# Six accumulator banks in the feed-forward loop, and the sample states' products placed in the output projection

## The chip, the cores and the metric

The kernel is written in Bass and runs on one core of one Trainium2 chip. A time is the device time of one execution in microseconds (us). The core has five instruction streams that run beside each other and wait for each other through semaphores: TensorE (PE, with its weight loads shown as PEld), VectorE (DVE), ScalarE (ACT), GpSimd (POOL) and SyncE (SP, which here only issues transfers). TensorE's granted clock has two levels, 2.4 GHz (shown as 1.00) and 1.2 GHz (shown as 0.50).

## The reference

One inference step of a decoder trunk with two layers, 1024 prompt tokens and 8 samples of 4 new tokens (1056 columns in all), model width 1024, feed-forward width 2816, all in fp32. Each layer computes

```
h = rmsnorm(x);  z = h @ w_in
o_gla = gated linear attention of 4 heads (key 64, value 128), with a recurrent state
o_swa = sliding-window attention of 8 query heads over 2 key/value heads
x = x + [o_gla ; o_swa] @ w_o
h = rmsnorm(x);  x = x + (silu(h @ w_gate) * (h @ w_up)) @ w_down
```

and a last rmsnorm gives the outputs. The gated linear attention also returns its recurrent states. For the prompt that is one state per layer. For the samples the new state of each sample is `exp(b_last) * S + k_dec^T v`, 8 samples by 4 heads of a 64 x 128 matrix. The sum `k_dec^T v` of these 32 small matrices is what the steps `sample_states` (the products) and `sample_sum` (scaling the old state and adding the products) compute. Nothing later in the layer reads these states: they are only stored.

## The kernel before, in words

All activations lie transposed, 128 channels by 1056 tokens, in eight channel tiles k = 0..7. The tokens are cut into three column tiles tt of 384, 384 and 288. A weight unit is 1024 x 128 weights (512 KB). SP loads it into `w_raw` (a ring of two), POOL splits it into a high part `w_hi` and a low part `w_lo` of reduced-precision fp32 (`split`, lines 481 to 506; the low part in pieces of 256 columns), and PE multiplies: for each k three matmuls, high x high, high x low, low x high (`passes`, lines 551 to 557). The activations are split the same way into `h_hi` (ACT) and `h_lo` (DVE, and for k = 1, 4, 7 POOL: `lows`, lines 508 to 515). So a product of one unit with one column tile is a group of 24 matmuls into one PSUM bank.

The order of all work up to the feed-forward part is written out by `schedule()` (lines 73 to 203) as a list of steps, and each engine walks through the same list and does its part of each step. The matmul groups are numbered in this order, group g writes bank `acc[g % 3]`, and `acc_free[b]` counts how often the reader of a bank has released it. `open_group` (line 547) makes PE wait for the release of the group three before.

PSUM has eight banks: `acc0` to `acc2`, `pair_a` (two banks), `pair_b` (two banks) and `single`. The last three serve the attention steps.

The list's end, around which the change lies:

- the output projection: units 19 to 26, three column tiles each. `("z", u, tt)` is PE's group, `("take", u, tt)` is DVE's addition of the bank to x (L1218), then ACT squares it (L858) and DVE adds the square to a running sum (L1158);
- the transition into the feed-forward part (lines 191 to 202): `stat` sums the squares over the channels on PE (L567), `rstd` turns that into 1/rms on ACT (L867, L870), `normed` makes the new h: DVE scales (L1178), ACT writes `h_hi` (L880), DVE or POOL write `h_lo` (L1183, L513). `sample_states` (PE, L793: 32 products with 32 rows, 64 output partitions and 128 columns, each recorded as two matmuls) stands between `stat` of tile 1 and `stat` of tile 2. `sample_sum` (DVE, L1430 and L1434) is the last step. It reads `pair_a` and `pair_b`. SP stores the result (L469) inside the feed-forward loads.

Then the feed-forward loop: 11 rounds (`Fori`, line 799 for PE). A round has 36 groups: four units (gate and up for two feed-forward tiles; 12 groups of 24 matmuls), then two units of w_down (24 groups of 6 matmuls). ACT reads a gate bank (Silu, L1128), DVE an up bank (L1483), DVE adds a w_down bank to x (L1498). Before each group `ff_open` (line 800) waits for the bank's last reader, with the numbering of `acc_free` carried on. In the first unit of the first round PE also waits, k by k, for the h of this column tile (`split_in`, line 812). POOL's order at this place (lines 530 to 538) is: split unit 27, lows of tiles 0 and 1, split unit 28, lows of tile 2, split unit 29.

Of the kernel before, what the change touches and what calls it, by code (L numbers as in the profile page):

```python
# [26 lines left out]
NTT = len(COLS)  # L27
TW = 384
RANK = 16
NCH = SEQ // P  # L30
# [12 lines left out]
POOL_LOWS = (1, 4, 7)  # L43
DVE_LOWS = tuple(k for k in range(KC) if k not in POOL_LOWS)
ACCS = 3
NEG = -1.0e30


# [2 lines left out]
UNITS = U_FF + 6 * FPAIRS  # L51
FF_UNITS = 6
FF_GROUPS = 4 * NTT + KC * NTT


CONSTS = {"ident": 128, "ones": 128, "band": 256, "reset": 32, "bmask": NB,
# [16 lines left out]
def schedule():  # L73
# [3 lines left out]
    steps = []  # L77
# [4 lines left out]
    def normed(n, tt, half=None):  # L82
        return [("normed", n, tt, h) for h in range(2) if half is None or h == half]

    def project(u, tt):
        return [("z", u, tt), ("take", u, tt)]
# [60 lines left out]
    gate = [(u, tt) for u in range(U_GG, U_WO) for tt in range(NTT)]  # L147
# [38 lines left out]
    for k in range(KC - 1):  # L186
        for tt in range(NTT):
            steps += project(U_WO + k, tt)
            if k > 0 or tt > 0:
                squares(1, (tt - 1) % NTT, [k if tt > 0 else k - 1])  # L190
    k, u = KC - 1, U_FF - 1
# [6 lines left out]
    steps += [("z", u, 2)] + normed(1, 0, 0) + [("stat", 1, 1), ("take", u, 2)]  # L198
    squares(1, 2, [k])

    steps += [("sample_states",), ("stat", 1, 2), ("rstd", 1, 1)] + normed(1, 0, 1) + [("rstd", 1, 2)]
    steps += normed(1, 1) + normed(1, 2) + [("sample_sum",)]
    return steps


# [23 lines left out]
def trunk(nc, x_t, units, consts, tables, dec_mask, params, w_gk2, state_in, kcache_t,  # L229
# [100 lines left out]
    pair_b = nc.alloc_psum_tensor("pair_b", [P, 1024], f32)  # L330
    single = nc.alloc_psum_tensor("single", [P, 512], f32)

    def sem(name):
        return nc.alloc_semaphore(name)

# [6 lines left out]

    acc_full = sem("acc_full")
    acc_free = [sem(f"acc_free{b}") for b in range(ACCS)]
    w_loaded = [sem(f"w_loaded{s}") for s in range(RING)]
    w_high = sem("w_high")
    ga_low = sem("ga_low")
# [62 lines left out]
    def bank(g):  # L410
        return acc[g % ACCS]

# [11 lines left out]
    def width(tt):  # L424
        return COLS[tt][1] - COLS[tt][0]
# [20 lines left out]
    with nc.Fori(0, DEPTH) as layer:  # L446
        with nc.Block() as block:
# [98 lines left out]
            def _(pe):  # L546
# [249 lines left out]
                        last.then_inc(ds_full, 1)  # L796


                with pe.Fori(0, FPAIRS) as i:
                    def ff_open(j):  # L800
                        g = G_FF + j
                        pe.wait_ge(acc_free[g % ACCS], i * (FF_GROUPS // ACCS) + g // ACCS)
                        return bank(g)

                    for j in range(4):
                        u = U_FF + j
                        pe.wait_ge(w_ready, i * FF_UNITS + (u + 1))
                        for tt in range(NTT):
                            out = ff_open(NTT * j + tt)[:, 0:width(tt)]
                            for k in range(KC):  # L810
                                if j == 0:
                                    split_in(pe, NTT + tt, k)
                                last = passes(out, u % RING, k, h_hi[:, k, cols(tt)], h_lo[:, k, cols(tt)],
                                              k == 0, k == KC - 1)
                            last.then_inc(acc_full, 1)
                    for j in range(2):
                        u = U_FF + 4 + j
                        pe.wait_ge(w_ready, i * FF_UNITS + (u + 1))
                        for tt in range(NTT):
                            pe.wait_ge(hid_ready, i * (2 * NTT) + (NTT + tt + 1))  # L820
                            for d in range(4):
                                out = ff_open(4 * NTT + 4 * (NTT * j + tt) + d)[:, 0:width(tt)]
                                for f in range(2):
                                    last = passes(out, u % RING, 4 * f + d, hid_hi[:, f, cols(tt)],
                                                  hid_lo[:, f, cols(tt)], f == 0, f == 1)
                                last.then_inc(acc_full, 1)

            @block.scalar
            def _(act):
# [290 lines left out]
                with act.Fori(0, FPAIRS) as i:  # L1120
                    for f in range(2):
                        for tt in range(NTT):
                            w = width(tt)
                            j = 2 * NTT * f + tt
                            g = G_FF + j
                            n_done = NTT * f + tt
                            act.wait_ge(acc_full, i * FF_GROUPS + (g + 1))
                            nc.scalar.activation(silu_g[:, tt, 0:w], bank(g)[:, 0:w], ACT.Silu)\  # L1128
                              .then_inc(acc_free[g % ACCS], 1)
                        for tt in range(NTT):  # L1130
                            w = width(tt)
                            n_done = NTT * f + tt
                            g = G_FF + NTT * (2 * f + 1) + tt
                            act.wait_ge(acc_free[g % ACCS], i * (FF_GROUPS // ACCS) + (g // ACCS + 1))
                            nc.scalar.activation(hid_hi[:, f, cols(tt)], tmp_a[:, n_done % 2, 0:w],  # L1135
                                                 ACT.Copy).then_inc(hid_high, 1)

# [3 lines left out]
            def _(dve):  # L1141
# [324 lines left out]
                with dve.Fori(0, FPAIRS) as i:  # L1466
                    for f in range(2):
                        for tt in range(NTT + 1):
                            if tt < NTT:
                                w = width(tt)  # L1470
                                j = NTT * (2 * f + 1) + tt
                                g = G_FF + j
                                n_done = NTT * f + tt
                                gate = g - NTT
                                dve.wait_ge(acc_free[gate % ACCS], i * (FF_GROUPS // ACCS) + (gate // ACCS + 1))
                                dve.wait_ge(acc_full, i * FF_GROUPS + (g + 1))
                                if n_done >= 2:
                                    dve.wait_ge(hid_ready, i * (2 * NTT) + (n_done - 1))
                                else:

                                    b = G_FF - 1
                                    dve.wait_ge(acc_free[b % ACCS], i * (FF_GROUPS // ACCS) + (b // ACCS + 1))
                                nc.vector.tensor_tensor(tmp_a[:, n_done % 2, 0:w], silu_g[:, tt, 0:w],  # L1483
                                                        bank(g)[:, 0:w], ALU.mult).then_inc(acc_free[g % ACCS], 1)
                            if tt > 0:
                                m = NTT * f + tt - 1
                                w = width(tt - 1)
# [4 lines left out]
                    for j in range(2):  # L1492
                        for tt in range(NTT):
                            for d in range(4):
                                g = G_FF + 4 * NTT + 4 * (NTT * j + tt) + d
                                dve.wait_ge(acc_full, i * FF_GROUPS + (g + 1))
                                xs = x[:, 4 * j + d, cols(tt)]
                                nc.vector.tensor_tensor(xs, xs, bank(g)[:, 0:width(tt)],  # L1498
                                                        ALU.add).then_inc(acc_free[g % ACCS], 1)

        nc.sync.sem_clear(layer_sems)
        nc.all_engine_barrier()
# [163 lines left out]
```

## Time and profile before

| what | value |
|---|---|
| time, median of 3 runs | 2704.58 us (2703.75 to 2707.66) |
| the profiled execution's own time | 2702.21 us |
| its span, first to last instruction | 2700.4 us |
| mean granted TensorE clock | 0.969 |
| PE busy | 2543.7 us, 94% |
| DVE, ACT, POOL busy | 1101.0, 583.3, 870.5 us (41%, 22%, 32%) |
| DMA | 128.66 MB, mean 48 GB/s |

Busy time is that of the records laid over each other, so PE, whose matmuls overlap, is not at its peak where it reads 94%. The span has two equal layers: in the first the output projection runs from about 453 to 551 us, the transition to 583 us, and the feed-forward loop from there to about 1350 us; in the second the transition ends at about 1918 us and the loop at 2674 us. The rest is the final norm and the store.

### The profile page before, as it was taken

The numbers are of one execution on the slowest core, as the hardware profiler recorded it, in microseconds if no ns is written. First come the engines' busy times: TensorE is split into PE (matmuls) and PEld (weight loads), VectorE is DVE, ScalarE is ACT, GpSimd is POOL, SyncE is SP. The second block draws the span as 40 slices with busy tenths as digits, with TensorE's granted clock in tenths as the row PEclk, the third lists the DMA queues.
The fourth block names the chain that finished last, engine by engine and source line by source line (L and its number), as shares of the span: only waits on it lengthen the run. The fifth ranks groups of instructions, "written<-read, shape, count | busy, mean of one in ns | idle before, by whom it ended". The sixth has DMA issues, their size and how long they took to land. (4 is left out here: it accounts for less than half of the span.)

```text
span 2700.4 us, 39407 instructions
## 1 busy us (share of the span) xinstructions
PE 2543.7 (94%) x15202; PEld 2404.5 (89%) x15202; DVE 1101.0 (41%) x2091; ACT 583.3 (22%) x1281; POOL 870.5 (32%) x1344
## 2 busy tenths in 40 slices
PE   3999989989999999999869999999899999999998
PEld 2887778989999999999858867789899999999997
DVE  6635386252222222222366354843522222222224
ACT  3035434130010100101130364441210101010012
POOL 3311112343333333333232211123433333333331
PEclk8999998989999999999969999999899999999999
DMA  4200011111111111111121001011111111111111
GB/s 146 92 24 24 18 38 51 47 47 47 47 39 47 47 47 47 42 43 47 47 97 41 24 24 39 17 64 42 48 47 47 47 47 39 47 47 47 47 39 71
DMA packets 47213, 128.66 MB, mean 48 GB/s; under 512 B 4272, under 2 KB 21872, under 8 KB 46320
## 3 DMA queue, kind: packets, MB, share of 16 engines
q1 hardware_dynamic: 38192, 110.91, 12.5%
q10 hardware_dynamic: 8928, 16.55, 1.7%
q8 instruction: 54, 0.88, 0.1%
q14 instruction: 39, 0.32, 0.0%
HBM read 116.10 MB, written 13.37 MB: 48 GB/s over the span
## 5 line engine op out<-in xcount | busy, mean ns | idle before, releaser
L555 PE MATMUL acc<-h_hi,w_hi 128*128 128x384 f32 (+1 forms) x3360 | 1121.2, 334 | 54.7 <-POOL h_lo L513 29.6
L556 PE MATMUL acc<-h_lo,w_hi 128*128 128x384 f32 (+1 forms) x3360 | 1100.4, 328 | 0.0
L557 PE MATMUL acc<-h_hi,w_lo 128*128 128x384 f32 (+1 forms) x3360 | 1097.9, 327 | 0.0
L555 PEld LDWEIGHTS acc<-h_hi,w_hi 128*128 128x128 f32 x3360 | 643.9, 192 | 95.4 <-issue 39.8
L556 PEld LDWEIGHTS acc<-h_lo,w_hi 128*128 128x128 f32 x3360 | 645.3, 192 | 0.6
L557 PEld LDWEIGHTS acc<-h_hi,w_lo 128*128 128x128 f32 x3360 | 644.1, 192 | 0.0
L487 POOL TENSOR_TENSOR w_hi<-w_raw,const 128x32 fp32r<-128x32 f32 x186 | 50.0, 269 | 1672.9 <-PE acc L557 1600.6
L495 POOL TENSOR_TENSOR w_lo<-w_raw,w_hi 128x256 fp32r<-128x256 f32 x744 | 545.2, 764 | 15.5
L1483 DVE TENSOR_TENSOR tmp_a<-silu_g,acc 128x384 f32<-128x384 f32 x132 | 68.8, 521 | 872.2 <-PE acc L557 872.2
L1498 DVE TENSOR_TENSOR x<-x,acc 128x384 f32<-128x384 f32 (+1 forms) x528 | 272.8, 520 | 203.5 <-PE acc L557 201.4
L555 PE MATMUL acc<-hid_hi,w_hi 128*128 128x384 f32 (+1 forms) x1056 | 342.4, 324 | 0.0
L556 PE MATMUL acc<-hid_lo,w_hi 128*128 128x384 f32 (+1 forms) x1056 | 340.9, 323 | 0.0
L557 PE MATMUL acc<-hid_hi,w_lo 128*128 128x384 f32 (+1 forms) x1056 | 340.4, 322 | 0.0
L1128 ACT ACTIVATE silu_g<-acc 128x384 f32<-128x384 f32 x132 | 61.2, 465 | 848.9 <-PE acc L557 848.8
L557 PEld LDWEIGHTS acc<-hid_hi,w_lo 128*128 128x128 f32 x1056 | 198.3, 188 | 0.0
L556 PEld LDWEIGHTS acc<-hid_lo,w_hi 128*128 128x128 f32 x1056 | 198.3, 188 | 0.0
L555 PEld LDWEIGHTS acc<-hid_hi,w_hi 128*128 128x128 f32 x1056 | 198.2, 188 | 0.0
L1135 ACT ACTIVATE hid_hi<-tmp_a 128x384 fp32r<-128x384 f32 x132 | 65.8, 499 | 468.5 <-DVE tmp_a L1483 468.5
L491 POOL TENSOR_SCALAR w_hi<-w_raw 128x512 fp32r<-128x512 f32 x186 | 134.5, 723 | 0.0
L489 POOL TENSOR_SCALAR w_hi<-w_raw 128x480 fp32r<-128x480 f32 x186 | 111.7, 601 | 0.0
L1489 DVE TENSOR_TENSOR hid_lo<-tmp_a,hid_hi 128x384 fp32r<-128x384 f32 x132 | 101.2, 792 | 0.0
L1273 DVE SCALAR_TENSOR_TENSOR prob<-pair_a,const 128x1024 f32<-128x1024 f32 (+1 forms) x32 | 36.8, 1151 | 139.4 <-PE pair_a L664 139.4
(187 smaller groups left out, 1854.2 us busy)
## 6 DMA issues: line engine op xcount, KB each, us to landing
w_raw<-units SPq DMA_DIRECT2D x186, 512.0 KB, 3.4
park<-x ACTq DMA_DIRECT2D x2, 2112.0 KB, 15.2
x<-park ACTq DMA_DIRECT2D x2, 2112.0 KB, 10.0
x<-x_t SPq DMA_DIRECT2D x2, 1536.0 KB, 9.2
y_t<-x SPq DMA_DIRECT2D x4, 768.0 KB, 3.5
rope<-tables SPq DMA_DIRECT2D x2, 1056.0 KB, 8.2
s<-state_in ACTq DMA_DIRECT2D x4, 512.0 KB, 6.1
state_s<-s SPq DMA_DIRECT2D x2, 1024.0 KB
```

The costliest lines, as they stand in the source:

```text
L487: nc.gpsimd.tensor_tensor(w_hi[:, s, 0:SUB], w_raw[:, s, 0:SUB], c_("ones")[:, 0:SUB], ALU.mult)
L489: nc.gpsimd.tensor_scalar(w_hi[:, s, SUB:UNIT // 2], w_raw[:, s, SUB:UNIT // 2], 1.0, 0.0, ALU.mult, ALU.add)
L491: nc.gpsimd.tensor_scalar(w_hi[:, s, UNIT // 2:], w_raw[:, s, UNIT // 2:], 1.0, 0.0, ALU.mult, ALU.add).then_inc(w_high, 1)
L495: low = nc.gpsimd.tensor_tensor(w_lo[:, s, a:a + LOW], w_raw[:, s, a:a + LOW], w_hi[:, s, a:a + LOW].bitcast(f32), ALU.subtract)
L555: nc.tensor.matmul(out, wh, hi, start=first, stop=False)
L556: nc.tensor.matmul(out, wh, lo, start=False, stop=False)
L557: return nc.tensor.matmul(out, wl, hi, start=False, stop=last)
L1128: nc.scalar.activation(silu_g[:, tt, 0:w], bank(g)[:, 0:w], ACT.Silu)\
L1135: nc.scalar.activation(hid_hi[:, f, cols(tt)], tmp_a[:, n_done % 2, 0:w], ACT.Copy).then_inc(hid_high, 1)
L1483: nc.vector.tensor_tensor(tmp_a[:, n_done % 2, 0:w], silu_g[:, tt, 0:w], bank(g)[:, 0:w], ALU.mult).then_inc(acc_free[g % ACCS], 1)
L1489: nc.vector.tensor_tensor(hid_lo[:, f, cols(tt - 1)], tmp_a[:, m % 2, 0:w], hid_hi[:, f, cols(tt - 1)].bitcast(f32), ALU.subtract).then_in ...
L1498: nc.vector.tensor_tensor(xs, xs, bank(g)[:, 0:width(tt)], ALU.add).then_inc(acc_free[g % ACCS], 1)
```

## The change

- The feed-forward loop takes six banks in turn: `acc0`, `acc1`, `acc2`, both halves of `pair_a`, and `single`. Group j of a round uses bank j % 6. Six new semaphores `ff_free[b]` count the releases. Before the loop PE waits for the last release of all three `acc` banks, for `s_ready` (the sample states' sum) and for `go_copied` (the last reader of `single`), and then raises each `ff_free` by one. ACT and DVE release to `ff_free`, and what waited for `acc_free` in the loop waits for `ff_free`.
- In the list, `sample_states` moves from the transition to behind group (20, 0) of the output projection, and `sample_sum` from the end of the list to behind group (21, 0).

POOL's splitting of the weights (low parts in pieces of 256 columns) is the same in both kernels.

```diff
@@ -43,6 +43,7 @@
 POOL_LOWS = (1, 4, 7)
 DVE_LOWS = tuple(k for k in range(KC) if k not in POOL_LOWS)
 ACCS = 3
+FF_ACCS = 6
 NEG = -1.0e30
 
 
@@ -51,6 +52,7 @@
 UNITS = U_FF + 6 * FPAIRS
 FF_UNITS = 6
 FF_GROUPS = 4 * NTT + KC * NTT
+FF_TURNS = FF_GROUPS // FF_ACCS
 
 
 CONSTS = {"ident": 128, "ones": 128, "band": 256, "reset": 32, "bmask": NB,
@@ -186,6 +188,10 @@
     for k in range(KC - 1):
         for tt in range(NTT):
             steps += project(U_WO + k, tt)
+            if k == 1 and tt == 0:
+                steps.append(("sample_states",))
+            if k == 2 and tt == 0:
+                steps.append(("sample_sum",))
             if k > 0 or tt > 0:
                 squares(1, (tt - 1) % NTT, [k if tt > 0 else k - 1])
     k, u = KC - 1, U_FF - 1
@@ -198,8 +204,8 @@
     steps += [("z", u, 2)] + normed(1, 0, 0) + [("stat", 1, 1), ("take", u, 2)]
     squares(1, 2, [k])
 
-    steps += [("sample_states",), ("stat", 1, 2), ("rstd", 1, 1)] + normed(1, 0, 1) + [("rstd", 1, 2)]
-    steps += normed(1, 1) + normed(1, 2) + [("sample_sum",)]
+    steps += [("stat", 1, 2), ("rstd", 1, 1)] + normed(1, 0, 1) + [("rstd", 1, 2)]
+    steps += normed(1, 1) + normed(1, 2)
     return steps
 
 
@@ -330,6 +336,8 @@
     pair_b = nc.alloc_psum_tensor("pair_b", [P, 1024], f32)
     single = nc.alloc_psum_tensor("single", [P, 512], f32)
 
+    ff_acc = [acc[0][:], acc[1][:], acc[2][:], pair_a[:, 0:512], pair_a[:, 512:1024], single[:]]
+
     def sem(name):
         return nc.alloc_semaphore(name)
 
@@ -342,6 +350,7 @@
 
     acc_full = sem("acc_full")
     acc_free = [sem(f"acc_free{b}") for b in range(ACCS)]
+    ff_free = [sem(f"ff_free{b}") for b in range(FF_ACCS)]
     w_loaded = [sem(f"w_loaded{s}") for s in range(RING)]
     w_high = sem("w_high")
     ga_low = sem("ga_low")
@@ -796,11 +805,16 @@
                         last.then_inc(ds_full, 1)
 
 
+                for b in range(ACCS):
+                    pe.wait_ge(acc_free[b], (G_FF - b + ACCS - 1) // ACCS)
+                pe.wait_ge(s_ready, NCH + 1)
+                pe.wait_ge(go_copied, NCH + 1)
+                for b in range(FF_ACCS):
+                    nc.tensor.sem_inc(ff_free[b], 1)
                 with pe.Fori(0, FPAIRS) as i:
                     def ff_open(j):
-                        g = G_FF + j
-                        pe.wait_ge(acc_free[g % ACCS], i * (FF_GROUPS // ACCS) + g // ACCS)
-                        return bank(g)
+                        pe.wait_ge(ff_free[j % FF_ACCS], i * FF_TURNS + (j // FF_ACCS + 1))
+                        return ff_acc[j % FF_ACCS]
 
                     for j in range(4):
                         u = U_FF + j
@@ -1125,13 +1139,13 @@
                             g = G_FF + j
                             n_done = NTT * f + tt
                             act.wait_ge(acc_full, i * FF_GROUPS + (g + 1))
-                            nc.scalar.activation(silu_g[:, tt, 0:w], bank(g)[:, 0:w], ACT.Silu)\
-                              .then_inc(acc_free[g % ACCS], 1)
+                            nc.scalar.activation(silu_g[:, tt, 0:w], ff_acc[j % FF_ACCS][:, 0:w], ACT.Silu)\
+                              .then_inc(ff_free[j % FF_ACCS], 1)
                         for tt in range(NTT):
                             w = width(tt)
                             n_done = NTT * f + tt
-                            g = G_FF + NTT * (2 * f + 1) + tt
-                            act.wait_ge(acc_free[g % ACCS], i * (FF_GROUPS // ACCS) + (g // ACCS + 1))
+                            j = NTT * (2 * f + 1) + tt
+                            act.wait_ge(ff_free[j % FF_ACCS], i * FF_TURNS + (j // FF_ACCS + 2))
                             nc.scalar.activation(hid_hi[:, f, cols(tt)], tmp_a[:, n_done % 2, 0:w],
                                                  ACT.Copy).then_inc(hid_high, 1)
 
@@ -1471,17 +1485,17 @@
                                 j = NTT * (2 * f + 1) + tt
                                 g = G_FF + j
                                 n_done = NTT * f + tt
-                                gate = g - NTT
-                                dve.wait_ge(acc_free[gate % ACCS], i * (FF_GROUPS // ACCS) + (gate // ACCS + 1))
+                                gate = j - NTT
+                                dve.wait_ge(ff_free[gate % FF_ACCS], i * FF_TURNS + (gate // FF_ACCS + 2))
                                 dve.wait_ge(acc_full, i * FF_GROUPS + (g + 1))
                                 if n_done >= 2:
                                     dve.wait_ge(hid_ready, i * (2 * NTT) + (n_done - 1))
                                 else:
 
-                                    b = G_FF - 1
-                                    dve.wait_ge(acc_free[b % ACCS], i * (FF_GROUPS // ACCS) + (b // ACCS + 1))
+                                    dve.wait_ge(ff_free[FF_ACCS - 1], i * FF_TURNS + 1)
                                 nc.vector.tensor_tensor(tmp_a[:, n_done % 2, 0:w], silu_g[:, tt, 0:w],
-                                                        bank(g)[:, 0:w], ALU.mult).then_inc(acc_free[g % ACCS], 1)
+                                                        ff_acc[j % FF_ACCS][:, 0:w],
+                                                        ALU.mult).then_inc(ff_free[j % FF_ACCS], 1)
                             if tt > 0:
                                 m = NTT * f + tt - 1
                                 w = width(tt - 1)
@@ -1492,11 +1506,11 @@
                     for j in range(2):
                         for tt in range(NTT):
                             for d in range(4):
-                                g = G_FF + 4 * NTT + 4 * (NTT * j + tt) + d
-                                dve.wait_ge(acc_full, i * FF_GROUPS + (g + 1))
+                                n = 4 * NTT + 4 * (NTT * j + tt) + d
+                                dve.wait_ge(acc_full, i * FF_GROUPS + (G_FF + n + 1))
                                 xs = x[:, 4 * j + d, cols(tt)]
-                                nc.vector.tensor_tensor(xs, xs, bank(g)[:, 0:width(tt)],
-                                                        ALU.add).then_inc(acc_free[g % ACCS], 1)
+                                nc.vector.tensor_tensor(xs, xs, ff_acc[n % FF_ACCS][:, 0:width(tt)],
+                                                        ALU.add).then_inc(ff_free[n % FF_ACCS], 1)
 
         nc.sync.sem_clear(layer_sems)
         nc.all_engine_barrier()
```

## Rows read from the trace of the kernel before

**Rows 1.** The page's part 1: busy us, share of the span, instructions.

```profile
PE 2543.7 (94%) x15202; PEld 2404.5 (89%) x15202; DVE 1101.0 (41%) x2091; ACT 583.3 (22%) x1281; POOL 870.5 (32%) x1344
```

**Rows 2.** Busy time by stretch: from:to, length; busy us by engine, granted clock, DMA.

```profile
463.00:547.00 84.00, 84.00 (x521) 84.00 (x520) 25.75 (x54) 14.66 (x34) 31.45 (x49) 1.00 0.18 62
...
547.00:584.00 37.00, 29.42 (x175) 25.93 (x174) 32.24 (x46) 18.01 (x36) 17.65 (x18) 0.77 0.00 0
...
584.00:1340.00 756.00, 754.69 (x4677) 754.46 (x4675) 217.33 (x397) 75.07 (x139) 278.06 (x447) 1.00 0.14 45
...
1882.00:1919.00 37.00, 29.26 (x174) 25.77 (x173) 32.77 (x46) 18.01 (x36) 17.59 (x19) 0.77 0.00 0
```

**Rows 3.** Timeline of PE: start, us, instruction, count, idle before it.

```profile
547.75 0.59 PE L555 MATMUL acc<-h_hi,w_hi 128*128 128x288 f32 x1
...
548.17 0.29 PE L556 MATMUL acc<-h_lo,w_hi 128*128 128x288 f32 x1
...
551.23 0.81 PE L567 MATMUL acc<-ssum,const 128*128 128x384 f32 x2
...
551.97 1.96 PE L793 MATMUL pair_a<-vo,kdm 32*64 32x128 f32 x32
...
553.77 2.33 PE L793 MATMUL pair_b<-vo,kdm 32*64 32x128 f32 x32
...
556.55 1.30 PE L567 MATMUL acc<-ssum_c,const 128*128 128x288 f32 x2 [0.46 <-DVE ssum_c L1158]
...
557.24 0.94 PE L555 MATMUL acc<-h_hi,w_hi 128*128 128x384 f32 x1
```

**Rows 4.** Busy time by stretch, single microseconds, columns as in Rows 2.

```profile
439.00:440.00 1.00, 1.00 (x5) 0.84 (x5) 0.00 (x0) 0.28 (x1) 0.00 (x0) 0.53 0.00 0
...
554.00:555.00 1.00, 1.00 (x24) 1.00 (x22) 0.88 (x3) 0.49 (x1) 0.00 (x0) 1.00 0.00 0
...
555.00:556.00 1.00, 1.00 (x14) 0.69 (x9) 0.49 (x3) 0.52 (x2) 0.00 (x0) 0.56 0.00 0
...
561.00:562.00 1.00, 1.00 (x5) 1.00 (x4) 1.00 (x1) 0.65 (x2) 0.68 (x1) 0.53 0.00 0
...
562.00:563.00 1.00, 1.00 (x8) 1.00 (x7) 1.00 (x3) 0.53 (x1) 0.27 (x1) 1.00 0.00 0
```

**Rows 5.** Timeline of PE, restart after a wait in unit 19.

```profile
459.77 0.69 PE L555 MATMUL acc<-h_hi,w_hi 128*128 128x384 f32 x1 [2.72 <-DVE h_lo L1456]
...
462.81 0.41 PE L555 MATMUL acc<-h_hi,w_hi 128*128 128x384 f32 x1
```

**Rows 6.** Timeline of PE, the last column tile of unit 27.

```profile
577.03 0.61 PE L555 MATMUL acc<-h_hi,w_hi 128*128 128x288 f32 x1 [4.46 <-POOL h_lo L513]
...
581.28 0.44 PE L557 MATMUL acc<-h_hi,w_lo 128*128 128x288 f32 x1
...
582.74 0.40 PE L555 MATMUL acc<-h_hi,w_hi 128*128 128x288 f32 x1 [1.01 <-POOL h_lo L513]
```

**Rows 7.** Timelines of ACT, DVE and POOL, the last h of tile 2.

```profile
579.49 0.44 ACT L880 ACTIVATE h_hi<-tmp_n 128x288 fp32r<-128x288 f32 x1 [0.52 <-DVE tmp_n L1178]
...
579.74 2.29 DVE L1430 TENSOR_TENSOR s<-s,small 128x2048 f32<-128x2048 f32 x1
...
576.20 1.54 POOL L513 TENSOR_TENSOR h_lo<-tmp_n,h_hi 128x288 fp32r<-128x288 f32 x2
...
580.01 2.67 POOL L513 TENSOR_TENSOR h_lo<-tmp_n,h_hi 128x288 fp32r<-128x288 f32 x1 [2.27 <-ACT h_hi L880]
```

**Rows 8.** Line L513: duration in ns, min/median/max.

```profile
L513 POOL TENSOR_TENSOR h_lo<-tmp_n,h_hi x36: 785/1072/2672, 27.8 to 1914.6; 128x384 fp32r<-128x384 f32 x24, 128x288 fp32r<-128x288 f32 x12
```

**Rows 9.** Timeline of ACT, reader of the last statistics bank.

```profile
560.27 0.48 ACT L867 ACTIVATE rstds<-acc,const 128x288 f32<-128x288 f32 x1
```

**Rows 10.** Timelines of DVE and POOL in the output projection.

```profile
489.50 0.55 DVE L1218 TENSOR_TENSOR x<-x,acc 128x384 f32<-128x384 f32 x1 [3.29 <-PE acc L557]
...
492.73 0.25 POOL L487 TENSOR_TENSOR w_hi<-w_raw,const 128x32 fp32r<-128x32 f32 x1 [7.01 <-PE acc L557]
```

## The prediction

> **What bounds the kernel now.** I read the page's busy times first, then busy time by stretch, then the timelines of the stretch around the moved steps. PE is busy 94% of the span, the next engine 41% [rows 1]. By stretch this is not even [rows 2]. In the output projection, 463 to 547 us, PE's records cover 84.00 of 84.00 us at clock 1.00. In the first layer's feed-forward loop, 584 to 1340 us, they cover 754.69 of 756.00 us at clock 1.00. Only the transition between them, 547 to 584 us, has room: 29.42 of 37 us, clock 0.77, and the second layer's transition, 1882 to 1919 us, is its copy. So what is added to PE in the projection lengthens the kernel at its full price, what is taken from PE in the transition is worth something only where PE ends a wait, and the loop has 1.3 us per layer to give at most.
>
> **Part 1, `sample_states` into the projection.** In the transition the block stands behind `stat` of tile 1. Its 64 recorded matmuls run from 551.97 us; 32 of them take 1.80 us (551.97 to 553.77), so 0.056 us each at clock 1.00 [rows 3]. After the block PE still waits 0.46 us for DVE's last addition before `stat` of tile 2 at 556.55 [rows 3]. So the end of that `stat` doesn't depend on the block: taking it out makes PE idle from 552.0 to 556.5 and gains nothing.
>
> At its new place, behind group (20, 0) at about 474 us, PE has no idle time, and the block costs:
> - 64 x 0.056 = 3.6 us;
> - the way back into the projection's products: after the fp32 matmuls of a `stat` the first product's successor starts 0.42 us later (547.75 to 548.17) where 0.13 us is the cadence within such a group (24 products in 3.2 us) [rows 3], so 0.3 us;
> - the way in: 551.23 to 551.97 is 0.74 us [rows 3], of which the two passes of `stat` over 384 columns are 0.35 (two products' cadence), so up to 0.4 us; between two groups of products it is 0. I take the middle, 0.2 us.
>
> Together 4.1 us per layer (3.9 to 4.3). Nothing later in the projection takes it back, since PE waits nowhere there until the transition. All other engines' work behind it moves with PE, because each `take` waits for its group.
>
> **Part 2, the clock around the block.** In this trace the granted clock falls to 1.2 GHz inside the block: 1.00 in 554 to 555 us, 0.56 in 555 to 556 us, with PE busy in every one of these microseconds, by these small products alone for the 3 us before [rows 4]. It reads 0.53 in 561 to 562 and 1.00 from 562 on. The same happens in 439 to 440 us (0.53) [rows 4], behind the other block of small sample products. So the block seems not to hold the clock. In the transition a low clock hides behind the waits for h; in the projection it is paid for. The nearest row for the price is a restart in the same projection: products from 459.77 us at 0.32 us each until 462.81 us, about 9.5 of them, against 0.176 at the full clock [rows 5], so 9.5 x 0.144 = 1.4 us. Bounds: 0, if the dense products right before and behind the block keep the clock up, and 3.1 us, if it stays low for as long as from 555.2 to 562 us (6.8 us, of which 0.144/0.32 = 45% is lost). I take 1.4 us per layer, by the nearest row.
>
> The Trainium skill (TensorE: Matmul & The Clock Gate, "What's actually happening" and the goals table) says that the clock follows how busy PE has been and falls back after PE has been idle. By that rule a block without a gap would not lower it. This trace doesn't agree: PE shows no gap from 552 to 555 us and the clock fell [rows 4]. By the rule the sum would be that of rival 1.
>
> **Part 3, `sample_sum` out of the transition.** The last thing that PE waits for in unit 27 is h_lo of tile 2, k = 7, made by POOL. ACT's high part is there at 579.93; POOL starts at 580.01 and needs 2.67 us, until 582.68, and PE goes on at 582.74 [rows 6, 7]. Other instructions of this line took as little as 0.785 us [rows 8]. Beside the slow one DVE runs the first instruction of `sample_sum`, 2.29 us from 579.74, the only DVE work at that moment [rows 7]. With it gone I expect POOL to be done at 580.01 + 0.785, so PE could go on at 580.86: 1.88 us earlier. But PE itself is then late. It works through k = 1 to 6 at the low clock, and the last of these 18 products starts at 581.28, 0.24 us per product, so the next slot is 581.52 [rows 6]: 1.22 us earlier. If the clock rises a little sooner, it is more. I take 1.5 us per layer (1.22 to 1.88).
>
> At its new place `sample_sum` is 2.29 us plus two additions over the same columns, 4.6 us together as an estimate. DVE has 3.29 us idle before the next `take` (489.50) [rows 10], so that `take` comes 1.3 us late, and the squares and their additions behind it too. Its bank is wanted only three groups, over 11 us, later, so PE doesn't see it. POOL's next split starts at 492.73, after 7.01 us idle [rows 10]; `sample_sum`, some 485.9 to 490.5 us on this clock, falls in the idle time. Cost 0. SP's store of the states waits for this sum and holds up the weight load behind it; now it finds the sum ready. POOL never waited for that load, so this is worth 0 too.
>
> **Part 4, the new wait at the loop's start.** Before, PE's first group of the loop needed only the bank three groups back and started at 557.24 [rows 3]. Now it needs all three banks, so also the one that ACT reads last, by L867 at 560.27 to 560.75 [rows 9]. With six increments it starts at about 561, 3.7 us later. Everything on PE is queued behind this, first the group of unit 27, tile 0. What hides it is the next wait: PE may not do k = 1 of tile 2 before 577.03, when POOL, which splits unit 28 first, has delivered [rows 6, 7]. Even if all 51 products of tiles 0 and 1 and k = 0 ran at the low clock, 48 x 0.32 + 3 x 0.24 = 16.1 us, PE would be there at 577.1. Cost 0; without that cover 3.7 us per layer. The waits for `s_ready` and `go_copied` are long fulfilled.
>
> **Part 5, six banks in the loop.** The longest reader of a w_down bank is far shorter than the two groups that lie between, and PE's records leave 1.3 us of 756 open [rows 2]. A ring of six has nothing to shorten: 0, at best 1.3 us per layer. The waits are as many as before. ACT's and DVE's orders don't change.
>
> **Sum.** Per layer 4.1 + 1.4 - 1.5 = +4.0 us; two layers +8.0 us. The profiled execution took 2702.21 us, 2.4 us under the median of the runs, so it would take 2710.2 us, and the median 2704.58 + 8.0 = 2712.6 us. What this kernel's measurement can tell from no change is 0.2%, 5.4 us.
>
> **The rivals.**
> 1. *The clock holds through the block.* At the new place, dense products stand directly before and behind it, while before there was a `stat` and a gap on one side and a wait on the other. Against it: the two falls of rows 4. Then the sum is 2 x (4.1 - 1.5) = +5.2 us, 2709.8 us, within what counts as no change. It decides as soon as the clock costs under 0.1 us per layer; from there on the answer is "no change" and not "slower".
> 2. *The clock stays low twice as long*, as behind 555 us: 2 x (4.1 + 3.1 - 1.5) = +11.4 us, 2716.0 us. For it: the block may spill over the fall, so that it rises a step later. Against it: the dense products start at once.
> 3. *Six banks do gain in the loop*: the whole 1.3 us per layer, 8.0 - 2.6 = +5.4 us, 2710.0 us. Against it: w_down's matmuls show no idle time in front of them.
> 4. *The new wait isn't hidden*, because the later restart keeps POOL or DVE back: 8.0 + 2 x 3.7 = +15.4 us, 2720 us. Against it: neither waits for a feed-forward group before 583 us.
> 5. *The block runs beside the neighbouring products*, since it uses only 32 rows and 64 columns of the array, and costs nearly nothing: 2 x (0.5 - 1.5) = -2 us, 2702.6 us. Against it: 0.056 us for each 128-column matmul is the rate of one stream, not of two.
>
> **How the numbers follow.** Chances: the forecast 0.50 (some of it with a fall of the clock in one layer only, 2711.2 us), rival 1 0.22, rival 2 0.12, rival 3 0.05, rival 4 0.05, rival 5 0.03, and 0.03 for something unnamed. Slower by over 0.2% are the forecast, rivals 2 and 4 and a little of 3: 0.70. Faster by over 0.2% would need part 3 at its best and a block at almost no cost: 0.04. The rest, 0.26, is no change. The range reaches from 2706 (rival 1 with the cheap ends of parts 1 and 3, 2 x (3.9 - 1.88) = +4.0, less what the runs scatter) to 2718 us (rival 2 with the same scatter).
>
> **What would show it.** In the trace after: L793 between 473 and 480 us with 3.6 to 4.5 us from its first start to the next product, and every later group of the projection later by 4.1 us or, with the clock's fall, 5.5 us; the granted clock under 1.00 in the 3 to 4 us behind the block; the last L513 of tile 2 at 0.8 to 1.1 us instead of 2.67; PE's first group of the loop behind L867; rounds of the loop as long as before. I am wrong if the projection doesn't grow, if the clock stays at 1.00 behind the block, or if the loop's rounds change.

## The result and the profile after

The changed kernel takes 2716.67 us (median of 5 runs, 2716.31 to 2720.45) against 2704.2 us (2703.75 to 2707.66): a ratio of 1.0048, with the 95% interval 1.0033 to 1.0063. That is slower, by 12.5 us or 0.5%, and the interval doesn't hold 1. The forecast was +8.0 us and 2712.6 us, so the direction was right, the time lies inside the range (2706 to 2718 us), and the size was too small by a third. The +8.0 us lie just under the interval (1.0033 is +8.9 us), and the same code run again below gives nearly the same value, so the gap has to be explained. Two executions among those below, 13976.57 us of the changed kernel and 5298.39 us of the kernel before, lie far outside all others and are in no ratio.

The page after, part 1, busy us and share of the span, to be read against [rows 1]:

```profile
PE 2550.7 (94%) x15202; PEld 2412.1 (89%) x15202; DVE 1102.2 (41%) x2091; ACT 583.5 (21%) x1281; POOL 867.8 (32%) x1344
```

The span is 2714.5 us and the time of the profiled execution 2716.31 us. Busy time by stretch, the projection behind unit 19, the transition and the loop of the first layer, against [rows 2]:

```profile
469.00:553.00 84.00, 84.00 (x563) 83.58 (x563) 26.75 (x46) 11.25 (x23) 31.48 (x49) 1.00 0.12 40
...
549.00:588.00 39.00, 26.32 (x132) 24.44 (x131) 29.23 (x45) 16.51 (x34) 17.34 (x20) 0.82 0.18 54
...
591.00:1347.00 756.00, 753.33 (x4669) 753.10 (x4667) 217.20 (x396) 75.09 (x139) 277.50 (x445) 1.00 0.13 43
```

Projection and loop read as before: PE covered throughout at clock 1.00 (in the loop 753.33 of 756.00 us, with 8 records fewer than in the stretch of before, while the rounds below are equal), so a longer time there is more work or slower work, not waiting. The transition has lost PE work (26.32 us in 39).

I cut both executions at the same points: the start of unit 20, of unit 21, of `stat` of tile 0, and w_down's first product in the loop (the 34.8 us of unit 28's to 30's products lie in the last piece; they have no wait). All in us:

| stretch | before, layer 1 / 2 | after, layer 1 / 2 |
|---|---|---|
| start of unit 20 to start of unit 21 (holds the block) | 11.62 / 11.62 | 15.48 / 18.54 |
| units 21 to 25 | 58.10 / 58.10 | 58.10 / 58.10 |
| start of unit 26 to `stat` of tile 0 | 8.43 / 8.43 | 8.43 / 8.43 |
| `stat` of tile 0 to w_down's first product | 70.69 / 70.78 | 68.83 / 69.81 |
| one round of the loop | 69.72 | 69.72 |
| first product to unit 20 of layer 1 (code the change doesn't touch) | 441.24 | 445.01 |
| w_down's first product in the last round of layer 1 to unit 20 of layer 2 (untouched too) | 488.48 | 487.97 |
| final norm, first matmul to the end | 15.55 | 18.52 |

The change acts in two rows only: unit 20 (+3.86 and +6.92 us) and the transition (-1.86 and -0.97 us). Together that is +8.0 us. The two profiled spans differ by 14.1 us (2700.4 and 2714.5); the other 6 us lie in code that is the same in both (+3.8, -0.5 and +3.0 us in the last three rows). So the +8.0 us of this one pair of profiles are no confirmation of the forecast's +8.0 us. The timeline of PE around the block, after, first in layer 1, then in layer 2 (start us, us, instruction, count):

```profile
476.94 0.34 PE L566 MATMUL acc<-h_hi,w_lo 128*128 128x384 f32 x1
...
477.20 1.96 PE L802 MATMUL pair_a<-vo,kdm 32*64 32x128 f32 x32
...
479.00 1.91 PE L802 MATMUL pair_b<-vo,kdm 32*64 32x128 f32 x32
...
480.84 0.45 PE L564 MATMUL acc<-h_hi,w_hi 128*128 128x384 f32 x1
...
481.13 0.34 PE L565 MATMUL acc<-h_lo,w_hi 128*128 128x384 f32 x1
...
1813.21 1.96 PE L802 MATMUL pair_a<-vo,kdm 32*64 32x128 f32 x32
...
1815.01 2.32 PE L802 MATMUL pair_b<-vo,kdm 32*64 32x128 f32 x32
...
1817.26 0.69 PE L564 MATMUL acc<-h_hi,w_hi 128*128 128x384 f32 x1
...
1817.75 0.52 PE L565 MATMUL acc<-h_lo,w_hi 128*128 128x384 f32 x1
```

In layer 1 the 64 matmuls start every 0.056 us and the first product comes 3.90 us behind the last one before the block. In layer 2 the block ends slower, and the products behind it start every 0.32 us (1817.75 and on) instead of 0.176. The granted clock of single microseconds (third column from the right) says why:

```profile
480.00:481.00 1.00, 1.00 (x19) 0.83 (x16) 0.00 (x0) 0.00 (x0) 0.00 (x0) 1.00 0.24 86
...
481.00:482.00 1.00, 1.00 (x6) 1.00 (x7) 0.00 (x0) 0.00 (x0) 0.00 (x0) 1.00 0.00 0
...
1815.00:1816.00 1.00, 1.00 (x23) 1.00 (x21) 0.00 (x0) 0.00 (x0) 0.00 (x0) 1.00 0.93 369
...
1816.00:1817.00 1.00, 1.00 (x18) 0.93 (x14) 0.00 (x0) 0.00 (x0) 0.00 (x0) 0.69 0.27 94
...
1817.00:1818.00 1.00, 1.00 (x6) 0.74 (x3) 0.00 (x0) 0.00 (x0) 0.00 (x0) 0.50 0.00 0
...
1822.00:1823.00 1.00, 1.00 (x5) 1.00 (x4) 0.00 (x0) 0.00 (x0) 0.00 (x0) 0.50 0.00 0
...
1823.00:1824.00 1.00, 1.00 (x7) 1.00 (x6) 0.00 (x0) 0.00 (x0) 0.00 (x0) 0.90 0.00 0
```

Layer 1 keeps 1.00 through the block; in layer 2 the clock falls in its last part (0.69, then 0.50) and is back only in 1823 to 1824 us. The transition, after, layer 1, PE with ACT's last read of a bank between, and then POOL's last low part, against [rows 6, 7]:

```profile
564.05 1.30 PE L576 MATMUL acc<-ssum_c,const 128*128 128x288 f32 x2 [4.51 <-DVE ssum_c L1172]
...
567.75 0.48 ACT L881 ACTIVATE rstds<-acc,const 128x288 f32<-128x288 f32 x1
...
569.58 0.66 PE L564 MATMUL acc<-h_hi,w_hi 128*128 128x384 f32 x1 [4.23 <-issue]
...
584.54 0.61 PE L564 MATMUL acc<-h_hi,w_hi 128*128 128x288 f32 x1 [3.94 <-POOL h_lo L522]
...
587.35 0.41 PE L566 MATMUL acc<-h_hi,w_lo 128*128 128x288 f32 x1
...
588.38 0.39 PE L564 MATMUL acc<-h_hi,w_hi 128*128 128x288 f32 x1
...
587.51 0.80 POOL L522 TENSOR_TENSOR h_lo<-tmp_n,h_hi 128x288 fp32r<-128x288 f32 x1 [2.27 <-ACT h_hi L894]
```

POOL needs 0.80 us where it needed 2.67, and PE starts the last k 1.03 us behind the last product of k = 6 (587.35 to 588.38). In layer 2:

```profile
1923.63 0.61 PE L564 MATMUL acc<-h_hi,w_hi 128*128 128x288 f32 x1 [4.40 <-POOL h_lo L522]
...
1928.59 0.44 PE L566 MATMUL acc<-h_hi,w_lo 128*128 128x288 f32 x1
...
1928.83 0.43 PE L564 MATMUL pair_a<-h_hi,w_hi 128*128 128x384 f32 x1
...
1926.60 0.80 POOL L522 TENSOR_TENSOR h_lo<-tmp_n,h_hi 128x288 fp32r<-128x288 f32 x1 [2.27 <-ACT h_hi L894]
```

Here POOL is done at 1927.40, but PE is at the low clock, its products 0.24 us apart up to 1928.83, and doesn't wait at all. The gain is what PE's clock leaves of it: 1.86 us in one layer, 0.97 us in the other.

### The profile page after: what moved, and what is told of

Same layout as the page of the kernel before. It is cut to its first block and busy times, and to the rows that moved or that the text cites. A ratio compares the mean times of both kernels' runs of the same rounds, so it can differ in the third digit from the quotient of the medians.

```text
span 2714.5 us, 39049 instructions
## 1 busy us (share of the span) xinstructions
PE 2550.7 (94%) x15202; PEld 2412.1 (89%) x15202; DVE 1102.2 (41%) x2091; ACT 583.5 (21%) x1281; POOL 867.8 (32%) x1344
## 3 DMA queue, kind: packets, MB, share of 16 engines
q1 hardware_dynamic: 38192, 110.91, 11.8%
## 5 line engine op out<-in xcount | busy, mean ns | idle before, releaser
L564 PE MATMUL acc<-h_hi,w_hi 128*128 128x384 f32 (+1 forms) x2304 | 779.5, 338 | 54.7 <-POOL h_lo L522 22.8
L565 PE MATMUL acc<-h_lo,w_hi 128*128 128x384 f32 (+1 forms) x2304 | 762.5, 331 | 0.0
L566 PE MATMUL acc<-h_hi,w_lo 128*128 128x384 f32 (+1 forms) x2304 | 760.4, 330 | 0.0
L564 PEld LDWEIGHTS acc<-h_hi,w_hi 128*128 128x128 f32 x2304 | 448.6, 195 | 93.1 <-issue 49.4
L565 PEld LDWEIGHTS acc<-h_lo,w_hi 128*128 128x128 f32 x2304 | 449.1, 195 | 0.3
L566 PEld LDWEIGHTS acc<-h_hi,w_lo 128*128 128x128 f32 x2304 | 448.0, 194 | 0.0
L564 PE MATMUL pair_a<-h_hi,w_hi 128*128 128x384 f32 x704 | 238.9, 339 | 0.0
L565 PE MATMUL pair_a<-h_lo,w_hi 128*128 128x384 f32 x704 | 237.1, 337 | 0.0
L566 PE MATMUL pair_a<-h_hi,w_lo 128*128 128x384 f32 x704 | 236.5, 336 | 0.0
L564 PE MATMUL acc<-hid_hi,w_hi 128*128 128x384 f32 x528 | 175.1, 332 | 0.0
```

The costliest lines, as they stand in the source:

```text
L564: nc.tensor.matmul(out, wh, hi, start=first, stop=False)
L565: nc.tensor.matmul(out, wh, lo, start=False, stop=False)
L566: return nc.tensor.matmul(out, wl, hi, start=False, stop=last)
```

## The experiments

All times are medians, ratios against the kernel before on the same chip, with their 95% interval.

**The move alone.** The old banks and numbering, both steps moved:

```diff
+            if k == 1 and tt == 0:
+                steps.append(("sample_states",))
+            if k == 2 and tt == 0:
+                steps.append(("sample_sum",))
...
-    steps += [("sample_states",), ("stat", 1, 2), ...
-    steps += normed(1, 1) + normed(1, 2) + [("sample_sum",)]
+    steps += [("stat", 1, 2), ...
+    steps += normed(1, 1) + normed(1, 2)
```

> Both steps are moved as in the change, but the loop keeps its three banks and its old numbering. Theory A (all of the 12.5 us comes with the move: the products on PE's path in the projection, and the clock behind them; the six banks and the longer wait at the loop's start give and cost nothing): within 2 us of the change, 2714 to 2719 us, rounds of the loop as long as in both kernels. Rival B (the six banks or the wait at the loop's start cost what part 1 to 3 of the prediction leave over, some 4 to 8 us): 2708 to 2712 us.

Measured: 2717.01 us (2712.89 to 2717.71), ratio 1.0037 (1.0024 to 1.0051). Unit 20 takes 17.01 and 18.54 us, `stat` of tile 0 to w_down 69.49 and 69.78 us, a round 69.72 us. PE starts the loop right behind the last `stat` (563.46):

```profile
564.14 0.94 PE L559 MATMUL acc<-h_hi,w_hi 128*128 128x384 f32 x1
```

Theory A holds: with three banks and without the long wait at the loop's start the time is that of the change. The interval alone (+6.5 to +13.8 us) wouldn't exclude the top of rival B; the stretches, which are those of the change, do.

**The banks alone.** Six banks, the steps at their old places (the schedule's part of the diff undone).

> Six banks, but sample_states and sample_sum at their old places, so PE can't start the loop before DVE's last step of the transition. Both theories: unit 27's 11.6 us of products, that ran beside the transition, come behind it, the first of them at the low clock: 12 to 15 us a layer, 2728 to 2734 us; after that rounds of 69.7 us as before. If the loop gained anything from six banks, rounds would be shorter here.

Measured: 2734.42 us, ratio 1.0104 (1.0088 to 1.0119). PE's first product of the loop:

```profile
584.27 1.21 DVE L1444 TENSOR_TENSOR s<-s,pair_b 128x1024 f32<-128x1024 f32 x1
...
587.08 0.66 PE L560 MATMUL acc<-h_hi,w_hi 128*128 128x384 f32 x1 [28.06 <-issue]
```

It starts 28 us after `stat` of tile 2, and 1.6 us behind the end of DVE's last step ("issue" in the row is read here as the wait for that step, since it ended last of what PE waits for). `stat` of tile 0 to w_down is 86.6 and 86.7 us instead of 70.7, so 15.9 us a layer, a little more than the 12 to 15 us expected; rounds stay at 69.72 us. So six banks need the move, and the loop gains nothing from them.

**Nearly no block.** The change with 1 of the 32 products:

```diff
-                        for b in range(NB):
-                            for hd in range(GH):
+                        for b in range(1):
+                            for hd in range(1):
```

> The change with 1 of the 32 products of sample_states (the stored sample states are then not the reference's). Theory A: the block's 3.85 us shrink to about 0.5 us and the clock has no reason to fall behind it; the gain of part 3 (1.9 us a layer) stays: 2 x (0.5 - 1.9) = -3 us against before, 2700 to 2703 us. Rival C (part of the 12.5 us has nothing to do with the block: other code of the change or other places of the clock's changes): 2705 to 2709 us.

Measured: 2704.39 us (2699.59 to 2706.44, 11 runs), ratio 0.9997 (0.9988 to 1.0006). Unit 20 takes 12.18 us in both layers (+0.56), the transition is 1.4 and 1.8 us shorter than before. The clock stays up around the product, which starts at 475.43 us in layer 1:

```profile
474.00:484.00 10.00, 10.00 (x63) 9.58 (x62) 2.08 (x5) 1.07 (x3) 2.11 (x5) 1.00 0.16 54
```

The median is 1 to 4 us above what I gave theory A, but the interval (-3.2 to +1.6 us) holds the -2.1 us that the two rows add up to, so it does not show rival C, nor exclude its lower end. What it does show: with one product instead of 32 the 12.5 us are gone. The block is the loss.

**The sum behind the last low part.** The kernel before with one wait:

```diff
                         dve.wait_ge(go_full, NCH + 1)
+                        split_in(dve, 2 * NTT - 1, POOL_LOWS[-1])
```

> The kernel before with one wait more: sample_sum on DVE waits until POOL has made the last low part of h (tile 2, k = 7). Nothing is moved. Theory A: POOL's instruction takes 0.8 us instead of 2.67 us, PE goes on 1.2 to 1.9 us earlier a layer, sample_sum still ends before DVE's first work of the loop: 2700 to 2702 us. Rival D (PE is itself late by its clock, or the sum then holds back the loop's first tmp_a): 2703 to 2705 us.

Measured: 2703.64 us (2700.01 to 2705.63, 11 runs), ratio 0.9995 (0.9986 to 1.0004): not told apart from no change. PE, the single microsecond from 1914 us (granted clock 0.50, third column from the right), POOL and DVE in its second transition:

```profile
1916.65 0.41 PE L555 MATMUL acc<-h_hi,w_hi 128*128 128x384 f32 x1 [0.32 <-ACT silu_g L1128]
...
1914.00:1915.00 1.00, 1.00 (x6) 1.00 (x5) 0.59 (x2) 0.73 (x2) 0.23 (x1) 0.50 0.00 0
...
1914.78 0.80 POOL L513 TENSOR_TENSOR h_lo<-tmp_n,h_hi 128x288 fp32r<-128x288 f32 x1 [2.27 <-ACT h_hi L880]
...
1915.71 2.29 DVE L1431 TENSOR_TENSOR s<-s,small 128x2048 f32<-128x2048 f32 x1 [1.12 <-POOL h_lo L513]
...
1921.14 0.55 DVE L1484 TENSOR_TENSOR tmp_a<-silu_g,acc 128x384 f32<-128x384 f32 x1 [0.75 <-PE acc L557]
```

POOL's instruction is down to 0.80 us, as in the change, so part 3's mechanism is shown alone, with nothing moved. The stretch from `stat` of tile 0 to w_down is 69.83 and 69.50 us, 0.9 and 1.3 us shorter than before. Rival D's first half is what happened: PE is late by its low clock. It doesn't wait for the low part that is ready at 1915.58; its own products, 0.24 us apart until 1915.09, bring it to k = 7 only at 1915.77. A new small wait stands beside it: the first group of unit 28 waits 0.32 us for ACT's first Silu, the reader of the bank three groups back, before which ACT shows a table load (ACT_TABLE_LOAD) of 1.28 us from 1914.71.

**The change again.**

> The changed kernel once more, for a second profile of it and more times. So far four layers with the moved block are profiled: group (20, 0) to (21, 0) took 15.5, 17.0, 18.5 and 18.5 us (11.6 before), by where the granted clock fell. Theory A (the block's price is 3.9 us at the full clock and up to 7 us where the clock falls behind it, and this varies from execution to execution with the place of the clock's changes): again a value from 15.5 to 18.5 us in each layer, with different falls elsewhere; time 2713 to 2720 us. Rival (the fall in the second layer only is a property of the program): the same 15.5 and 18.5 us as in the first profile.

Measured: 2716.37 us (median of the five executions from 2712.4 to 2717.98), ratio 1.0042 (1.0028 to 1.0055). Unit 20 takes 18.54 and 18.55 us. So the fall in the second layer only was no property of the program; here it stands in both. PE in layer 1, the block's second half, the first product and the last that was still slow (16 of them start 0.32 us apart):

```profile
477.17 2.44 PE L802 MATMUL pair_b<-vo,kdm 32*64 32x128 f32 x32
...
479.54 0.69 PE L564 MATMUL acc<-h_hi,w_hi 128*128 128x384 f32 x1
...
484.82 0.52 PE L565 MATMUL acc<-h_lo,w_hi 128*128 128x384 f32 x1
```

The transition takes 69.74 and 69.78 us, again with PE at the low clock in tile 2.

**The products in two halves.** 16 behind (20, 0), 16 behind (21, 0), the sum behind (22, 0):

```diff
-            if k == 1 and tt == 0:
-                steps.append(("sample_states",))
-            if k == 2 and tt == 0:
+            if k in (1, 2) and tt == 0:
+                steps.append(("sample_states", k - 1))
+            if k == 3 and tt == 0:
                 steps.append(("sample_sum",))
...
-                        for b in range(NB):
+                        for b in range(4 * s[1], 4 * s[1] + 4):
...
-                        last.then_inc(ds_full, 1)
+                        if s[1] == 1:
+                            last.then_inc(ds_full, 1)
```

> The change with the block cut in two: 16 products behind (20, 0), 16 behind (21, 0), the sum behind (22, 0). Theory A (the clock falls because the small products follow each other too long without a dense one between): no fall behind either half; each half costs 1.8 us and 0.45 us of way in and out, 4.5 us a layer instead of 3.9 to 6.9, so 2 to 4 us less than the change, 2712 to 2714 us. Rival B (the fall comes with any such product or not at all by them): the clock still falls, and the second way in and out comes on top, 2717 to 2719 us.

Measured: 2711.89 us (2709.01 to 2712.55), ratio 1.0028 (1.0017 to 1.0039), 4.5 us less than the change run again in the same series. PE in layer 1 (both halves, each with the first product behind it), and the stretch around them in either layer:

```profile
474.33 1.96 PE L802 MATMUL pair_a<-vo,kdm 32*64 32x128 f32 x32
...
476.22 0.45 PE L564 MATMUL acc<-h_hi,w_hi 128*128 128x384 f32 x1
...
488.06 1.96 PE L802 MATMUL pair_b<-vo,kdm 32*64 32x128 f32 x32
...
489.95 0.45 PE L564 MATMUL acc<-h_hi,w_hi 128*128 128x384 f32 x1
...
470.00:500.00 30.00, 30.00 (x225) 29.15 (x224) 6.50 (x12) 3.43 (x7) 10.92 (x18) 1.00 0.11 36
...
1800.00:1830.00 30.00, 30.00 (x224) 29.15 (x223) 8.26 (x22) 6.62 (x17) 8.72 (x14) 1.00 0.21 79
```

The granted clock is 1.00 over both stretches, and the projection has grown by 2.11 + 2.11 = 4.2 us in each layer. The same 32 products, with 11.8 us of dense ones between their halves, didn't bring the clock down in either layer, and the second way in and out costs 0.4 us. Theory A holds; the time is at the lower end of what it gave, because a half costs 2.1 us and not 2.25.

**Unit 28 split early, with the change.** POOL makes one low part of tile 0, splits unit 28, and then makes the others:

```diff
-                    if j == 0:
-                        lows(1, 0)
-                        lows(1, 1)
-                    elif j == 1:
-                        lows(1, 2)
+                    if j == 0:
+                        lows(1, 0, POOL_LOWS[:1])
+                    elif j == 1:
+                        lows(1, 0, POOL_LOWS[1:])
+                        lows(1, 1)
+                        lows(1, 2)
```

> The change, and POOL splits unit 28 behind the first low part of h of tile 0 instead of behind those of tile 1. So the wait of 4 to 5 us for POOL in tile 2 goes, which hid the late start of the loop. Theory A (that wait was the cover): PE starts the loop at the same place, behind ACT's last read, and runs the 72 products of unit 27 with h ready early, bounded by DVE's chain and by its own late start at the low clock: unit 28 starts 2 to 4 us earlier a layer, 2708 to 2713 us. Rival (DVE's chain ends as late as before, or POOL's split gets in the way of the next low parts): no gain, 2715 to 2718 us.

Measured: 2710.82 us (2709.51 to 2713.17), ratio 1.0028 (1.0018 to 1.0038). `stat` of tile 0 to w_down takes 67.62 and 67.72 us, 2.1 us less than with the change run again (1.2 and 2.1 us less than in its first profile). PE in the second layer: the loop's first product, and the only waits behind it; then the last scaling of DVE and the last low part of POOL:

```profile
1907.20 0.66 PE L565 MATMUL acc<-h_hi,w_hi 128*128 128x384 f32 x1 [5.68 <-issue]
...
1920.83 0.40 PE L565 MATMUL acc<-h_hi,w_hi 128*128 128x288 f32 x1 [1.22 <-POOL h_lo L522]
...
1922.93 0.40 PE L565 MATMUL acc<-h_hi,w_hi 128*128 128x288 f32 x1 [0.32 <-POOL h_lo L522]
...
1921.02 0.51 DVE L1193 SCALAR_TENSOR_TENSOR tmp_n<-x,par,rstds 128x288 f32<-128x288 f32 x1
...
1922.08 0.80 POOL L522 TENSOR_TENSOR h_lo<-tmp_n,h_hi 128x288 fp32r<-128x288 f32 x1 [1.30 <-ACT h_hi L895]
```

The wait of 4.40 us has become 1.22 and 0.32 us. The loop starts at 1907.20, 5.68 us after PE was last fed, and even now this late start isn't on the path: PE still has to wait for DVE's chain (scalings and its share of the low parts, with no idle time from 1899.35 to 1921.89 us), with ACT and POOL at its end.

**The same, with the kernel before** (three banks, nothing moved, and the wait of the fourth experiment).

> The kernel before (three banks, nothing moved) with the wait of the fourth experiment and unit 28's split placed as in the run just above. Theory A: with three banks PE starts the loop 3.7 us earlier than with the change, so it has only DVE's chain before it: unit 28 starts 4 to 6 us earlier a layer than in the kernel before, 2693 to 2697 us, faster than both kernels. Rival: DVE's chain, not POOL, sets the end, and the gain is 1 to 2 us a layer, 2700 to 2703 us.

Measured: 2700.06 us (2693.79 to 2703.45, 11 runs), ratio 0.9988 (0.9979 to 0.9996): faster than the kernel before by 3.2 us in the ratio (1.1 to 5.7), and so than both kernels. The gain per layer is 2.5 us (68.29 and 68.19 against 70.7), half of what I had expected. Two edits share it: the wait of the fourth experiment alone gave 0.9 and 1.3 us, so the earlier split adds 1.5 and 1.3 us. PE in the second layer, and POOL's last low part:

```profile
1901.29 0.41 PE L556 MATMUL acc<-h_hi,w_hi 128*128 128x288 f32 x1 [0.36 <-POOL h_lo L513]
...
1904.51 0.40 PE L556 MATMUL acc<-h_hi,w_hi 128*128 128x288 f32 x1 [1.28 <-POOL h_lo L513]
...
1906.61 0.40 PE L556 MATMUL acc<-h_hi,w_hi 128*128 128x288 f32 x1 [0.31 <-POOL h_lo L513]
...
1907.63 0.41 PE L556 MATMUL acc<-h_hi,w_hi 128*128 128x384 f32 x1 [0.36 <-ACT silu_g L1129]
...
1905.76 0.80 POOL L513 TENSOR_TENSOR h_lo<-tmp_n,h_hi 128x288 fp32r<-128x288 f32 x1 [1.30 <-ACT h_hi L881]
```

PE now stands in tile 2 for h part by part, 0.36, 1.28 and 0.31 us, each time for POOL, which is fed by ACT and DVE. That is the rival's mechanism. The fourth row is a wait for ACT's first Silu (0.36 us, and as much in the first layer). This wait, and the one of 0.32 us in the fourth experiment, are all that a ring of three banks costs PE in the transitions profiled.

## Why the prediction was right, and where it was short

**Part 1, the block's price: right.** 4.1 us a layer (3.9 to 4.3) were forecast, 3.86 us came where the clock held. The way out was right, the way in is about 0.1 us (476.94 to 477.20, against a cadence of 0.176); one product alone costs 0.56 us.

**Part 2, the clock: the term that was mis-sized.** I took 1.4 us a layer, by the restart at 459.77 us [rows 5], and kept 3.1 us as the far end and as rival 2. Of the eight layers profiled with the whole block behind (20, 0), six show +6.92 to +6.94 us in unit 20, one +5.39 and one +3.86. Less the block's own 3.86 us that is a clock price of 3.1 us in six, 1.5 us in one and none in one; the mean is 2.5 us. In the six the clock stays at 1.2 GHz for 6.8 us, as it did behind the block in the kernel before (555 to 562 us, [rows 4]). That was the nearer row: the same small products before the fall, and their tail behind it. I set it aside because dense products follow at once at the new place, and in six layers that didn't shorten it. Rival 2, at 2716.0 us, had the size; I gave it 0.12. The measured time lies in the range only because the range was stretched to rival 2, and the layer that came close to the 1.4 us (1.5 us) is one of eight.

**Part 3, the relief: right in mechanism, a little smaller.** The fourth experiment shows it alone. 1.5 us a layer were forecast (1.22 to 1.88); the six layers of the change and of the move alone give 1.91, 0.93, 1.25, 0.96, 1.00 and 0.96 us against the mean of 70.74 before, 1.2 us on average. Where the clock is low through all of tile 2, PE is on the path, not POOL.

**Parts 4 and 5: right.** The longer wait exists (569.58 is 1.35 us after ACT's last read ends), and costs nothing that the stretches show: the first experiment, without it, is no faster. It has a second cover that I hadn't named: with POOL's split out of the way, DVE's chain still ends too late for PE's late start to matter (the seventh experiment). The six banks leave the rounds at 69.72 us to the hundredth. `sample_sum` behind (21, 0) costs nothing: units 21 to 25 take 58.10 us with it and without.

**The sum.** 2 x (3.86 + 2.5 - 1.2) = +10.3 us from the measured terms, against +12.5 us in the medians; this lies inside both intervals of the change (+8.9 to +17 us, and +7.6 to +15 us the second time). What remains, some 2 us, isn't settled: the other code is the same in both. In the profiled executions those other stretches differ by more than that: in the ten of them 441 to 445 us up to unit 20 and 484.3 to 491.2 us from the last round of layer 1 to unit 20 of layer 2, and 3 us between them in the final norm. The places where the clock falls differ with them; that they are the whole reason isn't shown.

Rival 1 (the clock holds) came true in one layer of eight. Rivals 3, 4 and 5 did not appear.

## What to carry to other kernels

Before moving small work from a gap into a stretch where TensorE is the bound, price it twice: at its own length, and at the clock that the work behind it will get. Take the price of the clock from the place where the same instructions stood before (3.1 us here), not from a restart after a plain wait (1.4 us); and if they must be moved, cut them into pieces with dense products between. A buffer ring that no reader ever holds up gives nothing when it is doubled; look first at which wait ends last, here POOL's place in the order, where a reordering of a few lines took some 1.4 us a layer from the kernel before and about 2 us from the changed one, and 2.5 us a layer together with the later sum (3 us in the ratio).

## What the hardware showed that I had not expected

- 64 matmuls of 32 rows by 64 output partitions, one after the other for 3.6 us with PE shown busy throughout, brought the granted clock down in seven layers of eight. Two runs of 32 of them with 11.8 us of dense products between did not, in either of two layers. PE's busy time and its granted clock are two different things. Which property of these products matters (the rows, the output partitions or the fp32 type) no experiment here separates.
- The places where the clock changes differ between executions of one program: in the two profiles of the changed kernel it first falls at 41.4 and at 38.1 us, and identical code then takes 445.0 and 444.0 us up to unit 20, and 440.9 us in another kernel. The stretch between the layers' loops varies more, 484.3 to 491.2 us. So a single profile carries some 4 to 7 us of luck, a third to over a half of the effect studied here, and a difference of one stretch should be read at several layers or profiles.
- POOL's subtraction beside a DVE instruction that reads two large SBUF operands took 2.67 us (both layers of the kernel before and of the banks alone), and 0.79 to 0.81 us where the sum stood elsewhere (all eight other profiles).
